# Mean squares of a fused block kernel: one product with a matrix of 1/n and a logarithm-exponential factor, in place of token sums, square root, reciprocal and spread

## The chip, the cores and the metric

The kernel runs on one core of a Trainium2 chip. The metric is the device time of one execution in microseconds (us); less is better. Times of the kernel before are a median of three runs. TensorE (PE) multiplies matrices, VectorE (DVE), ScalarE (ACT) and GpSimd (POOL) work elementwise, and SyncE (SP) issues most of the transfers.

## The reference

Two transformer blocks stand one after the other, for one sequence of 512 tokens and 1024 channels, in float32. What matters here are their root mean square norms:

```python
def rmsnorm(t, g):
    y = t * lax.rsqrt(jnp.mean(t * t, axis=-1, keepdims=True) + EPS)   # EPS = 1e-6
    return y * g
```

They stand at these places:

- the first block's input norm (not touched here)
- a norm without weights of each of the 4 retention heads over its 512 value channels ("r")
- the first block's second norm, ahead of its feed-forward part ("n2")
- the first block's final norm over 1024 channels, and right behind it the second block's input norm ("n3" and "n3x"; see below)
- a norm of each of the 4 heads of the gated linear attention (GLA) over 128 channels ("g")
- the second block's norm ahead of its feed-forward part ("n4")
- the final norm (not touched here)

Around the norms stand projections of 1024 by 1024 and more, stick-breaking attention, retention, GLA, an attention over selected keys, and two gated feed-forward parts.

## The kernel before

**Layout.** Activations lie with channels on the 128 partitions and tokens along the free dimension: a tile is 128 channels by 512 tokens. A norm's sum over channels is then a sum over partitions, which TensorE makes, and the factor of each token must stand on all 128 partitions to multiply such tiles.

**Products.** Each big product is computed from operands split in a high and a low part: three matmuls of 512 columns (lines L1468, L1469, L1471) for each weight tile of 128 by 128. The weights are read in blocks into three buffers `stg` by SP. ScalarE rounds half a block into `wh` (L2223, 128x1024), and VectorE or GpSimd subtracts it into `wl` (L1767, L2578). A `split` in the order is this pair. Matmuls on plain float32 tiles stand in the trace as two records each.

**Order.** The class `Plan` writes one list of operations by hand-set rules, and every engine executes its own items of that list in order, with semaphores between engines. Foreground jobs are the big products. Side work is written as generators (`retain` for a retention head, `factors3` for n3 and n3x, `gla`, `turn_x` for n4) that advance one `yield` at a time between the weight tiles of the products: a stage has a rate, such as 0.55 or 1.1 steps for each tile. `rest(m)` or `pause=m` lets m such steps go by. `norm2` has no such cover: the next product is of the normed tile itself.

**A norm before.** ScalarE or GpSimd and VectorE have squared and added the channel tiles into one or two tiles of 128x512.

1. TensorE sums over partitions with the squares as stationary operand: four matmuls of one column (`token_sums` at L1570 for r and g; `sums` at L1602 and L1606, once for the accumulated tile and once for the last tile). The result is one value for each token, tokens on partitions, 128x4.
2. `sprd`: ScalarE loads the table of square roots (L2332) and takes the root of 128x4 (L2345), VectorE takes the reciprocal (L1888) and writes four diagonal tiles of 128x128 (L1895).
3. `sprdm`: TensorE multiplies them with a matrix of ones, four matmuls of 128 columns (L1585), which puts the factor on all partitions of a bank.
4. The readers: `rn` (L1901), `n2` (L1943), `x3` (L2010), `gn` (L2107); for n3 and n4 `rt` (L2003) copies the factor into the tile `RT`, by which the next products are multiplied as they leave their banks.

n3 folds two norms: `m1` makes the first one's mean times EPS, and the factor of the second follows from both sums. `tmt` (L2441) wants n3's factor with tokens on partitions, `rt3`, a copy of the 128x4 value.

**Around n2.** The order there is: squares of the last tile, `sums`, `sprd`, `sprdm`, `a2` (a small VectorE operation, L1934), a block's load, one `split`, and then `n2` and `n2_low` for the eight channel tiles (L1943 on VectorE, L2206 on ScalarE, L1954 on VectorE). The first product follows as its operands come.

**Around g.** The generators of the key selection (`best`, L2053 and L2055 on VectorE, ending with `chosen`, L2059) and of the GLA are interleaved; the attention (`al` at L1697) follows.

Of the kernel before, what the change touches and what calls it, by code (L numbers as in the profile page):

```python
# [55 lines left out]
def constants():  # L56
# [13 lines left out]
    mats = np.stack([np.eye(P), np.ones((P, P)),  # L70
                     ((s <= t) & (s // 64 == t // 64)).astype(float)], 1)
# [6 lines left out]
class Plan:  # L78
# [6 lines left out]
    def __init__(self):  # L85
# [5 lines left out]
        self.of = {}  # L91
# [158 lines left out]
def make_plan():  # L250
# [105 lines left out]

    def attend(pr):
# [9 lines left out]

        def rest(m):
            for _ in range(m):
                yield  # L370
# [104 lines left out]
    def spread(key, n, pause=0):  # L475
        emit("sprd", key, n)
        p.of["sprd", key] = p.counts["sprd"]
        for _ in range(pause):
            yield
        emit("sprdm", key)  # L480

    def retain(hh):
# [14 lines left out]
        take("O", ("r", hh), 2)  # L497
        emit("rsum", hh)
        yield from spread(("r", hh), 512, pause=6)
        yield  # L500
# [84 lines left out]
    def sums(which, f):  # L585


        emit("square", which, f)
        if f == KT - 1:
            def add():  # L590
                take("O", which)
                emit("sums", which)
            p.later.append([1, add])
# [35 lines left out]
    def norm2():  # L629
        p.flush()  # L630
        for _ in spread("n2", D):
            pass
# [120 lines left out]
    def factors3():  # L753
        yield
        yield
        p.flush()
        emit("m1")
        yield from spread("n3", D, pause=7)
        emit("rt", "n3")
# [3 lines left out]
        take("O", "n3x")  # L763
        yield from spread("n3x", D, pause=7)
# [77 lines left out]
    def gla():  # L842
        def rest(m):
            for _ in range(m):
                yield

# [37 lines left out]
        for r in range(2):  # L884
# [8 lines left out]
            for hh in range(2):  # L893
# [11 lines left out]
                take("O", ("g", hd), 2)  # L905
                emit("gsum", hd)
                yield from spread(("g", hd), P, pause=5)
                yield
# [144 lines left out]
    def turn_x():  # L1053
# [3 lines left out]
        yield from spread("n4", D, pause=10)  # L1057
        emit("rt", "n4")
# [23 lines left out]
v_set cact ada pe_ada a_x v_x v_a1 a_n1 sba sbr v_rot p_rot v_rs a_rsq p_rsq a_spread v_spread v_rn v_gr  # L1082
a_sq v_sq pe_sum v_a2 v_n2 v_m1 v_extra v_x3 v_sc v_best a_gb v_gc a_gd v_gd a_ge p_gf a_gg p_gh a_gh p_gi
# [16 lines left out]
def program(nc, a, out, scratch):  # L1100
# [8 lines left out]
    with base:  # L1109
# [8 lines left out]
        matf = sb("matf", [P, 2, P])  # L1118
# [7 lines left out]
        ONES, ONEC = matf[:, 0, :], matf[:, 0, 0:1]  # L1126
# [11 lines left out]
        m1c, m1s, top8, decs, fs, fd, fr = (cell(n) for n in (4, 4, 8, 16, 8, 4, 4))  # L1138
        mx, nmx, rsm = cell(32), cell(32), cell(32)
        vw = [(cell(4), cell(4)) for _ in range(2)]  # L1140
# [15 lines left out]
        with ExitStack() as ph:  # L1156
# [4 lines left out]
            with ExitStack() as ph1:  # L1161
# [4 lines left out]
                rdiag = sb("rdiag", [P, S], ctx=ph1)  # L1166
# [101 lines left out]
        def diag_of(key):  # L1268
            if isinstance(key, tuple):
                return rdiag if key[0] == "r" else tmp9  # L1270
            return TMP[6]

        def sums_of(key):
            ob = BANK[7]
            if isinstance(key, tuple):
                return ob[:, 0:4]
            if key == "n3x":
                return m1s
            return ob[:, 4:8] if key == "n3" else ob[:, 0:4]
# [74 lines left out]
        def sync(eng):  # L1354
# [6 lines left out]
            def row_load(k):  # L1361
# [5 lines left out]
                if k == 2:  # L1367
                    nc.sync.dma_start(matf[:, :, :], a["k_mats"][:, 1:3, :]).then_inc(s["d_matf"], 16)
# [40 lines left out]
        def tensor(eng):  # L1409
# [157 lines left out]
            def token_sums(key, sq):  # L1567
                ob = free(pe, key)
                for i in range(4):
                    t = T.matmul(ob[:, i:i + 1], sq[:, i * P:(i + 1) * P], ONEC, start=True, stop=True)  # L1570
                t.then_inc(fill(key), 1)

            def rsum(hh):
                pe.wait_ge("p_rsq", 3 * (hh + 1))
                token_sums(("r", hh), SQ)

            def gsum(hd):
                pe.wait_ge("a_gsq", hd + 1)
                token_sums(("g", hd), tmp8)

            def sprdm(key):
                ob, dg = free(pe, key), diag_of(key)
# [1125 lines left out]
```

## Time and profile before

| | us |
|---|---|
| median of three runs | 1940.64 (1938.31 to 1940.73) |
| the profiled execution, its device time | 1939.97 |
| its span, first to last instruction | 1938.2 |
| PE busy | 1894.5 |
| VectorE busy | 883.9 |
| ScalarE busy | 676.5 |
| GpSimd busy | 515.8 |

The mean granted TensorE clock of the profiled execution is 0.991 of full speed. The span is the profile's, and what is worked out below in microseconds of the span is taken off the device time of the same execution, which is 1.8 us longer than its span.

### The profile page before, as it was taken

Reading aid. Unit: us, or ns where it says so; the run is one execution under the profiler, and the core shown is the slowest. Engines: PE = TensorE matmul, PEld = TensorE weight load, DVE = VectorE, ACT = ScalarE, POOL = GpSimd, SP = SyncE. Lnnn points to the kernel's source line nnn. Section 1 sums busy time; section 2 is a strip of 40 time slices with the busy share of each in tenths; the row PEclk is TensorE's granted clock in tenths of the full one; section 3 lists DMA queues with packets and bytes.
Section 4 is the critical chain, followed back from the end, with each engine's and each line's share of the span. In section 5 each row is a group of like instructions: output and inputs, shape, how many; then the busy total and the mean of one; then the engine's idle time right before and its main releaser. Section 6 shows DMA issues by size and latency. Waiting matters only on the chain.

```text
span 1938.2 us, 21970 instructions
## 1 busy us (share of the span) xinstructions
PE 1894.5 (98%) x8837; PEld 1486.7 (77%) x8837; DVE 883.9 (46%) x1416; ACT 676.5 (35%) x1009; POOL 515.8 (27%) x285
## 2 busy tenths in 40 slices
PE   7999999999999999989999999999999999999998
PEld 6777778877777778877888888877676778888886
DVE  6466542655261314343333333557477654423433
ACT  5555541223232322433222223425336432212223
POOL 3433334444353533410000000134245311100100
PEclk9999999999999999989999999999899999999999
DMA  9411214534442123324323222423112132322321
GB/s 300 139 45 65 66 66 142 173 112 150 131 143 96 66 87 109 103 71 126 104 82 111 90 84 77 118 77 97 44 57 78 52 98 88 108 87 87 105 91 44
DMA packets 182332, 192.35 MB, mean 99 GB/s; under 512 B 10154, under 2 KB 166192, under 8 KB 181976
## 3 DMA queue, kind: packets, MB, share of 16 engines
q1 hardware_dynamic: 179704, 180.71, 29.2%
q0 software_dynamic: 1104, 5.24, 1.0%
q10 hardware_dynamic: 1424, 5.00, 0.7%
q8 instruction: 71, 1.16, 0.3%
q14 instruction: 29, 0.24, 0.0%
HBM read 188.82 MB, written 4.72 MB: 100 GB/s over the span
## 4 chain that ended last, share of the span: by engine, by line
PE 88%; DVE 8%; ACT 2%; issue 1%; POOL 1%; DMA 0%; DVEq 0%; SPq 0%; ACTq 0%; POOLq 0%
PE bank L1468 24%; PE bank L1471 23%; PE bank L1469 23%; PE bank L1490 2%; PE bank L1489 2%; PE bank L1488 2%; PE bank L1564 2%; DVE left L1827 2%; PE bank L1498 1%; PE bank L1534 1%; PE bank L1550 1%; PE bank L1514 1%; DVE ADA L1785 1%; PE bank L1450 1%; PE bank L1451 1%
## 5 line engine op out<-in xcount | busy, mean ns | idle before, releaser
L2578 POOL TENSOR_TENSOR wl<-stg,wh 128x1024 fp32r<-128x1024 f32 x150 | 364.6, 2432 | 865.3 <-ACT wh L2223 865.2
L1468 PE MATMUL bank<-hH,wh 128*128 128x512 f32 x1264 | 521.3, 412 | 2.8 <-DVE hL L1954 2.5
L1471 PE MATMUL bank<-hH,wl 128*128 128x512 f32 x1264 | 503.1, 398 | 0.0
L1469 PE MATMUL bank<-hL,wh 128*128 128x512 f32 x1264 | 502.9, 398 | 0.0
L2223 ACT ACTIVATE wh<-stg 128x1024 fp32r<-128x1024 f32 (+2 forms) x292 | 298.5, 1024 | 286.7 <-PE bank L1471 204.9
L1468 PEld LDWEIGHTS bank<-hH,wh 128*128 128x128 f32 x1264 | 239.9, 190 | 72.0 <-issue 19.3
L1471 PEld LDWEIGHTS bank<-hH,wl 128*128 128x128 f32 x1264 | 239.4, 189 | 58.1
L1469 PEld LDWEIGHTS bank<-hL,wh 128*128 128x128 f32 x1264 | 240.5, 190 | 51.1 <-issue 0.7
L1767 DVE TENSOR_TENSOR wl<-stg,wh 128x1024 fp32r<-128x1024 f32 (+2 forms) x142 | 168.1, 1186 | 238.0 <-ACT wh L2223 237.5
L1468 PE MATMUL bank<-h2H,wh 128*128 128x512 f32 x352 | 140.9, 400 | 0.0
L1471 PE MATMUL bank<-h2H,wl 128*128 128x512 f32 x352 | 140.2, 398 | 0.0
L1469 PE MATMUL bank<-h2L,wh 128*128 128x512 f32 x352 | 140.2, 398 | 0.0
L2626 POOL TENSOR_TENSOR tmp<-tmp,SQ 128x512 f32<-128x512 f32 x22 | 28.5, 1296 | 298.0 <-ACT tmp L2407 298.0
L1785 DVE SCALAR_TENSOR_TENSOR ADA<-stg,small,ADA 128x256 f32<-128x256 f32 x112 | 79.7, 712 | 3.4
L1471 PEld LDWEIGHTS bank<-h2H,wl 128*128 128x128 f32 x352 | 66.7, 190 | 16.2
L1468 PEld LDWEIGHTS bank<-h2H,wh 128*128 128x128 f32 x352 | 66.7, 190 | 15.8
L1469 PEld LDWEIGHTS bank<-h2L,wh 128*128 128x128 f32 x352 | 66.6, 189 | 15.9
L1971 DVE TENSOR_TENSOR tmp<-bank,tmp 128x512 f32<-128x512 f32 x44 | 30.4, 691 | 91.3 <-PE bank L1471 91.3
L1471 PE MATMUL bank<-fHa,wl 128*128 128x512 f32 x176 | 69.8, 396 | 0.0
L1468 PE MATMUL bank<-fHa,wh 128*128 128x512 f32 x176 | 69.8, 396 | 0.0
L1469 PE MATMUL bank<-fLa,wh 128*128 128x512 f32 x176 | 69.8, 396 | 0.0
L1827 DVE TENSOR_TENSOR_SCAN left<-tmp,masks 128x384 f32<-128x384 f32 (+2 forms) x64 | 61.9, 998 | 0.0
(328 smaller groups left out, 2616.4 us busy)
## 6 DMA issues: line engine op xcount, KB each, us to landing
stg<-in_w_in SPq DMA_DIRECT2D x54, 1024.0 KB, 5.2
stg<-in_w_ffn_in SPq DMA_DIRECT2D x22, 1024.0 KB, 5.1
stg<-in_w_ada SPq DMA_DIRECT2D x16, 1024.0 KB, 5.3
stg<-in_w_ffn_gate SPq DMA_DIRECT2D x11, 1024.0 KB, 5.2
stg<-in_w_ffn_up SPq DMA_DIRECT2D x11, 1024.0 KB, 5.3
stg<-in_w_ffn_down SPq DMA_DIRECT2D x10, 1024.0 KB, 5.0
stg<-in_w_ada SPq DMA_DIRECT2D x16, 512.0 KB, 6.2
stg<-in_w_proj_ret SPq DMA_DIRECT2D x8, 1024.0 KB, 5.0
```

What stands on the lines that cost most here:

```text
L1468: T.matmul(ps, wh, xh, start=j["first"] and k == 0, stop=False)
L1469: T.matmul(ps, wh, xl, start=False, stop=False)
L1471: t = T.matmul(ps, wl, xh, start=False, stop=j["stop"] and last)
L1488: T.matmul(gb[:, :], xh, wh, start=s0, stop=False)
L1489: T.matmul(gb[:, :], xh, wl, start=False, stop=False)
L1490: t = T.matmul(gb[:, :], xl, wh, start=False, stop=s1)
L1564: t = T.matmul(cb[:, j * P:S], v[:, j, d * P:(d + 1) * P], TMP[4 + n][:, off:off + w], start=j == 0, stop=j == 3)
L1767: V.tensor_tensor(lo, src, hi, ALU.subtract).then_inc(s["w_lo_dve"], 1)
L1785: V.scalar_tensor_tensor(last, view[:, k, :], cact[:, k:k + 1], acc, ALU.mult, ALU.add).then_inc(s["ada"], 1)
L1827: t = V.tensor_tensor_scan(left[:, back], tt[:, back], masks[:, 3, back], 1.0, ALU.mult, ALU.add)
L2223: A_.activation(hi, src, ACTF.Copy).then_inc(s["w_hi"], 1)
L2578: G.tensor_tensor(lo, src, hi, ALU.subtract).then_inc(s["w_lo_pool"], 1)
```

## The change

The constant `ones` becomes three constant matrices filled with 1/1024, 1/512 and 1/128. One matmul of 512 columns with such a matrix as stationary operand and the squares as moving operand puts the mean square of each token on all 128 partitions of a bank. Where `sums` had two groups of four one-column matmuls for each tile of squares, it has two such matmuls. The factor is then `exp(-0.5 * ln(mean + EPS))`: two ScalarE operations over 128x512, the first from the bank into a tile (`rlog`, `tmp9`, TMP[6] or TMP[4]), the second back into the bank, or for n3 and n4 straight into `RT`, so `rt` goes. `sprd`, `sprdm`, the reciprocal and the diagonals go. The table of both functions is loaded explicitly for r and g; for n2, n3 and n4 ahead of time, behind the square of channel tile 6. `m1` becomes two VectorE operations over 128x512. `rt3` is made by four one-column matmuls on `RT` and a small ScalarE copy. n3x takes a bank of its own (ring C), and `rt3` one of ring Z. The pauses in the order change as shown.

```diff
-    mats = np.stack([np.eye(P), np.ones((P, P)),
-                     ((s <= t) & (s // 64 == t // 64)).astype(float)], 1)
+    means = [np.full((P, P), 1.0 / n) for n in (D, 512, P)]
+    mats = np.stack([np.eye(P), *means, ((s <= t) & (s // 64 == t // 64)).astype(float)], 1)
...
     def retain(hh):
-        take("O", ("r", hh), 2)
+        take("O", ("r", hh))
         emit("rsum", hh)
-        yield from spread(("r", hh), 512, pause=6)
-        yield
+        yield from rest(2)
+        factor(("r", hh))
+        yield from rest(2)
...
     def norm2():
         p.flush()
-        for _ in spread("n2", D):
-            pass
+        factor("n2")
...
     def factors3():
         p.flush()
+        yield from rest(4)
         emit("m1")
-        yield from spread("n3", D, pause=7)
-        emit("rt", "n3")
+        yield
+        factor("n3")
         give("n3")
         p.known.add("r2")
         yield
-        take("O", "n3x")
-        yield from spread("n3x", D, pause=7)
+        factor("n3x")
+        yield from rest(2)
+        take("Z", "rt3")
+        emit("rt3")
+        give("rt3")
...
     def gla():
-                yield from spread(("g", hd), P, pause=5)
-                yield
+                yield from rest(2)
+                factor(("g", hd))
+                yield from rest(2)
...
     def turn_x():
-        yield from spread("n4", D, pause=10)
-        emit("rt", "n4")
+        yield from rest(3)
+        factor("n4")
...
             def rsum(hh):
+                pe.wait_ge("d_matf", 16)
                 pe.wait_ge("p_rsq", 3 * (hh + 1))
-                token_sums(("r", hh), SQ)
+                ob = free(pe, ("r", hh))
+                T.matmul(ob[:, :], MEAN[512], SQ[:, :], start=True, stop=True).then_inc(fill(("r", hh)), 1)
...
             def rt3_(*_):
+                zb = free(pe, "rt3")
+                emptied(pe, "n3")
                 for i in range(4):
+                    t = T.matmul(zb[:, i:i + 1], RT[:, i * P:(i + 1) * P], ident[:, 0:1], start=True, stop=True)
...
             def sums(which):
+                for ob, (acc, _) in zip(banks, SQS[which]):
+                    T.matmul(ob[:, :], MEAN[D], acc[:, :], start=True, stop=False)
                 pe.wait_ge("a_sq", squared(which, KT - 1))
+                for key, ob, (_, tt) in zip(keys, banks, SQS[which]):
+                    T.matmul(ob[:, :], MEAN[D], tt[:, :], start=False, stop=True).then_inc(fill(key), 1)
...
             def m1():
+                m = TMP[6][:, :]
+                V.tensor_scalar(m, filled(ve, "n3x")[:, :], EPS, EPS * EPS, ALU.mult, ALU.add).then_inc(s["v_m1"], 1)
+                ve.wait_ge("v_m1", 1)
+                V.tensor_tensor(m, filled(ve, "n3")[:, :], m, ALU.add).then_inc(s["v_m1"], 1)
...
+            def factor(key):
+                if isinstance(key, tuple):
+                    A_.preload_act_table_set("natural_log_exp_and_others")
+                log = log_of(key)
+                if key == "n3":
+                    ac.wait_ge("v_m1", 2)
+                    A_.activation(log[:, :], log[:, :], ACTF.Ln).then_inc(s["a_log"], 1)
+                else:
+                    ob = filled(ac, key)
+                    A_.activation(log[:, :], ob[:, :], ACTF.Ln, bias=e6).then_inc(s["a_log"], 1)
+                ac.wait_ge("a_log", of["log", key])
+                if key == "n3" or key == "n4":
+                    A_.activation(RT[:, :], log[:, :], ACTF.Exp, scale=-0.5).then_inc(empty(key), 1)
+                else:
+                    A_.activation(ob[:, :], log[:, :], ACTF.Exp, scale=-0.5).then_inc(s["a_log"], 1)
```

## Rows read from the trace of the kernel before

**Rows 1.** The page: busy time by engine; the chain that ended last, by engine.

```profile
PE 1894.5 (98%) x8837; PEld 1486.7 (77%) x8837; DVE 883.9 (46%) x1416; ACT 676.5 (35%) x1009; POOL 515.8 (27%) x285
PE 88%; DVE 8%; ACT 2%; issue 1%; POOL 1%; DMA 0%; DVEq 0%; SPq 0%; ACTq 0%; POOLq 0%
```

**Rows 2.** Busy us (count) by stretch: PE, PEld, DVE, ACT, POOL; clock, DMA, GB/s.

```profile
24.00:60.00 36.00, 35.86 (x174) 29.55 (x173) 24.77 (x63) 19.72 (x30) 25.96 (x18) 1.00 1.01 286
400.00:740.00 340.00, 337.52 (x1490) 264.43 (x1490) 128.09 (x210) 101.35 (x136) 148.40 (x73) 1.00 0.32 106
857.00:872.00 15.00, 10.09 (x43) 8.44 (x42) 10.87 (x20) 7.41 (x10) 0.00 (x0) 0.66 0.19 66
1242.00:1256.00 14.00, 14.00 (x76) 12.15 (x76) 5.81 (x20) 7.05 (x9) 6.13 (x3) 0.88 0.30 96
1362.00:1382.00 20.00, 18.01 (x62) 12.91 (x62) 6.28 (x14) 4.81 (x7) 2.35 (x1) 0.66 0.17 53
1552.00:1564.00 12.00, 11.06 (x54) 9.00 (x53) 6.99 (x13) 6.08 (x7) 0.00 (x0) 0.86 0.46 148
```

**Rows 3.** The chain around retention head 0: start us, us, what.

```profile
400.74 1.72 PE bank L1550 x4
...
425.98 0.79 PE bank L1570 x8
...
433.89 0.89 PE bank L1585 x8
```

**Rows 4.** The timeline around n2: start us, us, engine, operation, idle before.

```profile
858.45 0.63 ACT L2388 ACTIVATE tmp<-XR 128x512 f32<-128x512 f32 x1 [3.99 <-DVE XR L1930]
...
859.09 1.28 ACT L2332 ACT_TABLE_LOAD   x1
...
859.13 1.05 PE L1606 MATMUL bank<-small,tmp 128*128 128x1 f32 x8 [0.72 <-ACT tmp L2388]
860.39 0.26 ACT L2345 ACTIVATE small<-bank,small 128x4 f32<-128x4 f32 x1
860.55 1.05 ACT L2223 ACTIVATE wh<-stg 128x1024 fp32r<-128x1024 f32 x1
860.68 0.18 DVE L1888 RECIPROCAL small<-small 128x4 f32<-128x4 f32 x1 [2.27 <-ACT small L2345]
860.90 0.87 DVE L1895 TENSOR_SCALAR tmp<-ident,small 128x128 f32<-128x128 f32 x4
...
861.76 1.22 DVE L1767 TENSOR_TENSOR wl<-stg,wh 128x1024 fp32r<-128x1024 f32 x1
...
861.83 2.08 PE L1585 MATMUL bank<-tmp,matf 128*128 128x128 f32 x8 [1.65 <-DVE tmp L1895]
863.94 1.41 DVE L1943 SCALAR_TENSOR_TENSOR tmp<-XR,small,bank 128x512 f32<-128x512 f32 x2 [0.96 <-PE bank L1585]
```

**Rows 5.** The chain behind n2: products at half and at full clock.

```profile
867.64 0.43 PE bank L1471
...
871.09 0.23 PE bank L1471
```

**Rows 6.** Groups of ScalarE by form: one wide operation from a bank, one from SBUF.

```profile
L2487 ACT ACTIVATE tmp<-bank 128x512 f32<-128x512 f32 x4 | 2.4, 600 | 23.8 <-PE bank L1684 23.8
...
L2461 ACT ACTIVATE tmp<-tmp 128x512 f32<-128x512 f32 x2 | 1.3, 634 | 0.1
```

**Rows 7.** The chain at the sums of n3.

```profile
1242.91 1.68 PE bank L1602 x16
1244.59 2.03 PE bank L1606 x16
```

**Rows 8.** The chain at the first GLA head.

```profile
1374.46 1.50 PE bank L1570 x8
```

**Rows 9.** The timeline where the attention begins.

```profile
1441.83 2.06 DVE L2059 TENSOR_SCALAR SW<-SW 128x512 f32<-128x512 f32 x1
...
1444.70 0.70 PE L1697 MATMUL bank<-KA,QA 64*128 64x256 f32 x4 [1.23 <-DVE small L2122]
```

More of the change, by code:

```diff
@@ L355, in make_plan, with rest @@
     stage()
+    def rest(m):
+        for _ in range(m):
+            yield
     def attend(pr):
@@ L473, in rg_after @@
             p.fore.append(retain(hh))
[L475 to L478, printed above, removed]
-            yield
-        emit("sprdm", key)
+    def factor(key):
+        p.logs += 1
+        p.of["log", key] = p.logs
+        if key not in ("n3", "n4"):
+            p.logs += 1
+            p.of["factor", key] = p.logs
+        emit("factor", key)
     def retain(hh):
@@ L591, in add @@
                 take("O", which)
+                if which == "n3":
+                    take("C", "n3x")
                 emit("sums", which)
@@ L1266, in fkey, with log_of @@
             return ("f" + tag, t // FA), t % FA
-        def diag_of(key):
+        def log_of(key):
             if isinstance(key, tuple):
[L1270 to L1279, printed above, removed]
+                return rlog if key[0] == "r" else tmp9
+            return TMP[4 if key == "n3x" else 6]
         def fm_of(name, e):
@@ L1595, in sums @@
             def sums(which):
-                ob = free(pe, which)
-                pe.wait_ge("v_set", 2)
+                keys = ["n3x", "n3"] if which == "n3" else [which]
+                banks = [free(pe, key) for key in keys]
                 pe.wait_ge("v_sq", added(which, KT - 2))
-                for g, (acc, _) in enumerate(SQS[which]):
-                    for i in range(4):
-                        T.matmul(ob[:, 4 * g + i:4 * g + i + 1], acc[:, i * P:(i + 1) * P], one, start=g == 0 and i == 0, stop=False, skip_group_check=True)
+                for ob, (acc, _) in zip(banks, SQS[which]):
+                    T.matmul(ob[:, :], MEAN[D], acc[:, :], start=True, stop=False)
                 pe.wait_ge("a_sq", squared(which, KT - 1))
-                for g, (_, tt) in enumerate(SQS[which]):
-                    for i in range(4):
-                        t = T.matmul(ob[:, 4 * g + i:4 * g + i + 1], tt[:, i * P:(i + 1) * P], one, start=False,
-                                     stop=i == 3 and g == len(SQS[which]) - 1, skip_group_check=True)
-                t.then_inc(s["pe_sum"], 1)
+                for key, ob, (_, tt) in zip(keys, banks, SQS[which]):
+                    T.matmul(ob[:, :], MEAN[D], tt[:, :], start=False, stop=True).then_inc(fill(key), 1)
             def bias():
@@ L1878, in rvv, with factor @@
                 V.tensor_tensor(RG[:, d, :], cb[:, :], RG[:, d, :], ALU.mult).then_inc(empty(("rvv", hh, d)), 1)
[L1880 to L1895 removed]
+            def factor(key):
+                ve.wait_ge("a_log", of["factor", key])
+                return BANK[bank[key][0]]
             def rn(hh, d):
                 key = ("r", hh)
[L1899 removed]
+                rsb = factor(key)
                 emptied(ve, ("rvv", hh, d))
@@ L2104, in gn @@
                 key = ("g", hd)
-                rsb = filled(ve, key, 1)
+                rsb = factor(key)
                 emptied(ve, ("go", hd))
```

101 lines of the change are left out of this document (28 added, 73 removed).

## The prediction

> **What bounds the kernel now.** I read the page first: TensorE is busy for 1894.5 of 1938.2 us and holds 88% of the chain that ended last [rows 1]. So time on TensorE counts nearly one for one, and time on ScalarE or VectorE counts only where TensorE waits for it. Next I read the windows by stretch, because they show where TensorE is not at its full rate. In the retention stage (400 to 740 us) it is busy 337.5 of 340 us at clock 1.00; around n2, at n3, in the GLA and at n4 the granted clock falls to means of 0.66, 0.88, 0.66 and 0.86 [rows 2]. The half level is 1.2 GHz, the full one 2.4. Last I read the chain and the timeline at each norm: what a norm costs TensorE, and, for n2, who waits for whom.
>
> A product's matmul takes 0.43 us at half clock and 0.23 to 0.24 at full [rows 5], so of each us at half clock 0.45 us is lost. The time at half clock in a stretch is twice its length times (1 - mean clock): 2 x 14 x 0.12 = 3.4 us at n3, 2 x 12 x 0.14 = 3.4 us at n4, 2 x 20 x 0.34 = 13.6 us in the GLA, 2 x 15 x 0.34 = 10.2 us around n2 [rows 2].
>
> **The price of the new product.** A plain float32 matmul of 512 columns is priced by the scores of a retention head: two of them, on full tiles, take 1.72 us on the chain [rows 3], so 0.86 us each. The old four one-column matmuls take 0.79 us and the spread's four of 128 columns 0.89 us [rows 3].
>
> **Retention heads.** 0.79 + 0.89 - 0.86 = 0.82 us less of TensorE each, 3.3 us for four. TensorE has no slack there, so this counts in full. ScalarE gets a logarithm from a bank (0.60 us) and an exponential (0.63 us) [rows 6] for a root of 0.26 us [rows 4], about 1 us more per head; the table loads stay one per head. ScalarE is busy for 101 of 340 us in this stage [rows 2], which hides it. VectorE loses a reciprocal and four diagonals, 0.18 + 0.87 = 1.05 us at the least [rows 4]. If TensorE had waits to fill there, the gain could be anything down to nothing; the busy share says it has almost none.
>
> **GLA heads.** The same, 0.82 us, for three. The first head's sum ran at half clock, 1.50 us [rows 8]; there 1.50 + 0.89 - 2 x 0.86 = 0.67. Together 3.1 us.
>
> **n2, the only norm without cover.** I follow the chain. The last square ends at 859.08. Before, one-column matmuls, root, reciprocal, diagonals and spread follow, and the first `n2` starts at 863.94 [rows 4]. Now the last tile's matmul starts at 859.13 as before (the accumulated tile's one is done by then: TensorE had 0.72 us to wait for that square [rows 4], and 0.86 us is hardly more than the narrow group it replaces), and ends at about 860.2, with 0.2 us for its drain. Logarithm 0.60 and exponential 0.63 end at 861.45. If `n2` came then, 2.4 us would be won. But the order puts one `split` ahead of `n2`, and every engine is in order. Before, ScalarE rounded `wh` at 860.55 while VectorE was still at the reciprocal, and VectorE did `wl` from 861.76 to 862.98, under the spread matmuls (861.83 to 863.91) [rows 4]: both halves were free. Now ScalarE reaches `wh` only behind the exponential: 861.45 + 1.05 = 862.5, and VectorE's `wl`, which stands ahead of the first `n2` in its queue, ends at 863.7. So the first `n2` starts at about 863.7, and 0.2 us is won instead of 2.4. If the new matmul runs at half clock it is 0.86 us longer: 0.6 us lost. Bounds: -0.6 to +2.4, I take +0.2. The half clock behind n2 stays; I take it as it was. The table load of 1.28 us [rows 4], moved behind square 6, lies under a product of 24 x 0.235 = 5.6 us; without that cover it would cost its 1.28 us.
>
> **n3 and n3x.** Sums before: 1.68 + 2.03 = 3.71 us [rows 7], and two spreads, 1.78 us. Now four wide matmuls, 3.44 us, and four one-column ones for `rt3`, 0.79 us. 3.71 + 1.78 - 3.44 - 0.79 = 1.3 us less. The longer chain of `m1` (two wide VectorE operations) and four ScalarE operations is hidden under the next product, which does not need `RT` until its end, 5.6 us later; what is left over would cost what it overruns.
>
> Then the clock. Between 1242 and 1256 us TensorE is busy in all 14.00 us, and still the clock fell [rows 2]; the engine had just done 3.7 us of one-column matmuls [rows 7]. In the retention stage, with the float32 matmuls of up to 512 columns, it stood at 1.00 throughout. The new sums are such matmuls, so I expect the clock to stand. Of the 3.4 us at half clock, 0.7 us is in the 2.03 us already counted (2.03 - 1.68 is half of it); the other 2.7 us give back 2.7 x 0.45 = 1.2 us. n3 together: 2.5 us, bounds 1.3 and 2.5.
>
> **n4.** The spread's 0.89 us [rows 3] goes. Of the sums, the accumulated tile's matmul lies ahead of the wait for the last square, as before, and the last tile's takes about what the four narrow ones did. The clock fell behind these sums too: 3.4 x 0.45 = 1.5 us to be given back. Together 2.4 us, bounds 0.9 and 2.4.
>
> The Trainium skill bears on these two clock terms. Its page TensorE: Matmul & The Clock Gate, section on HAM oscillation, puts the fall down to stretches in which the engine idles. The trace does not agree at n3, where TensorE shows no idle time at all. By that rule n4, which keeps its short waits for the squares, would not be cured; that is rival 1.
>
> **Start of the attention.** The key selection ends with `chosen`, 1441.83 to 1443.89, and the second item of the attention waited 1.23 us for VectorE [rows 9]. The last two GLA heads no longer put 1.05 us or more each on VectorE ahead of it, 2.1 us, while TensorE arrives 1.6 us earlier by its own savings; later waits of the same kind shrink too. Fewer steps also pull the last selection steps forward in the order. I take 1.0 us, bounds 0 and 2.5.
>
> **The larger constant.** The load of the matrices grows from 128 to 256 KB at a time when the DMA share is 1.01 at 286 GB/s [rows 2]: 131 KB at that rate are 0.46 us. From 24 to 60 us TensorE is busy 35.9 of 36.0, so it does not wait for these transfers. I take 0, at most 0.46.
>
> **The sum.** 3.3 + 3.1 + 0.2 + 2.5 + 2.4 + 1.0 = 12.5 us. The profiled execution took 1939.97 us (span 1938.2), so 1927.5. The median is 0.67 above that execution: 1928.1. I say 1928.
>
> **Rivals.**
>
> 1. *The clock falls anyway at n3 and n4*, as the waits and the narrow `rt3` matmuls stay, and n2 meets the half clock with its wide matmul. The sum loses 1.2 + 1.5, 0.8 at n2 and the 1.0 of the attention: 8.0 us, so about 1932.5. For it: the clock also fell in stretches with waits, in the GLA. Against it: at n3 there was none, only narrow work.
> 2. *The GLA gets its clock back sooner.* The 13.6 us at half clock cost 6.1 us, and the first head's one-column sum lies in them, at 1374 [rows 8]. Without it the clock may return sooner; also what begins the fall comes at another moment. Worth 3 to 6 us: 1922 to 1925.
> 3. *Slower: the half clock of the GLA lasts on.* Its stretches of small matmuls are now met at other moments; if the clock, once down, stays down past 1382, each us costs 0.45. It decides from 12.5 / 0.45 = 28 us more, and up to the attention at 1441.8 [rows 9] (60 us more) it would cost 27 us, so up to 1955. Against it: on the same work the clock came back after 13.6 us before.
> 4. *TensorE's savings turn into waits* for ScalarE or VectorE, since ScalarE now sits in each norm for 1.28 + 0.60 + 0.63 us [rows 4, 6] and `rn` and `gn` come after fewer steps. VectorE would stand in front of other banks' readers. That gives 1936 to 1942. Against it: ScalarE's share of 35% [rows 1].
> 5. *The change doesn't do what it says*: logarithm and exponential each want a table load of their own, and the early load is lost. It shows in full only at n2, 2 x 1.28 = 2.6 us [rows 4]: 1930.5. The Trainium skill (ScalarE: Activation LUTs, section on table sets) has both functions in one set; in this trace the exponential and logarithm of the GLA's gates follow each other with 0.1 us between them [rows 6], so it agrees.
>
> **How the numbers follow.** Forecast 0.53 (with rival 5, 0.03, inside its own range 1924.5 to 1931), rival 1 0.18, rival 2 0.14, rival 4 0.07, rival 3 0.05. The range 1922 to 1934 leaves out rivals 3 and 4 and a third of rival 2, with a little of rival 1. About 0.2% (3.9 us) is what a measurement of this kernel can tell from no change. Faster: 0.53 + 0.03 + 0.18 + 0.14 and a little of rival 4, 0.89. Same: 0.06. Slower: 0.05.
>
> **What would show it.** In the new profile: the mean matmuls at about 0.86 us on the chain; clock 1.00 behind the sums of n3 and n4; at n2 exponential, `wh`, `wl`, `n2` in a row with no idle time between them, and TensorE idle from 860.2 relative until the first product; retention with no wait of TensorE. It would be wrong with a clock lower in the GLA than 0.66 or for longer, with TensorE waiting behind `gn` or `rn`, or with more table loads than the code asks for.

## The result

| | before | after |
|---|---|---|
| median, us | 1940.28 (four runs, 1938.31 to 1940.73) | 1922.47 (four runs, 1922.06 to 1923.94) |
| the profiled execution, device time | 1939.97 | 1923.94 |
| its span | 1938.2 | 1922.1 |
| its mean granted clock | 0.991 | 0.993 |

The ratio of after to before is 0.9912 (95% interval 0.9894 to 0.9929): 17.8 us less by the medians, 16.0 us by the two profiled executions. The forecast was 12.5 us less (1928.0), and the range 1922 to 1934 holds the result near its low end. So the sign is right and about 4 us of the profiled execution, over 5 us of the median, are to be found beside the forecast.

The page of after, the rows that answer to [rows 1]:

```profile
PE 1879.3 (98%) x8653; PEld 1463.2 (76%) x8653; DVE 868.0 (45%) x1352; ACT 687.2 (36%) x1021; POOL 516.4 (27%) x285
PE 87%; DVE 8%; ACT 2%; issue 2%; POOL 1%; DMA 0%; ACTq 0%; DVEq 0%; SPq 0%; POOLq 0%
```

TensorE lost 15.2 us of busy time and is still the bound; VectorE lost 15.9 us and ScalarE gained 10.7 us. The windows of after, at the places that answer to [rows 2] (columns: stretch, length, busy us and count of PE, PEld, DVE, ACT, POOL, then clock, DMA share, GB/s):

```profile
400.00:740.00 340.00, 338.86 (x1457) 263.14 (x1456) 126.57 (x194) 106.11 (x140) 151.81 (x74) 1.00 0.33 108
857.00:872.00 15.00, 12.16 (x44) 9.71 (x45) 11.17 (x17) 5.72 (x8) 0.00 (x0) 0.77 0.00 0
1234.00:1248.00 14.00, 13.79 (x57) 9.74 (x56) 9.85 (x15) 8.84 (x13) 6.21 (x3) 1.00 0.32 95
1353.00:1374.00 21.00, 18.87 (x60) 12.48 (x59) 5.75 (x10) 6.32 (x9) 2.35 (x1) 0.67 0.16 51
1536.00:1548.00 12.00, 11.15 (x46) 7.84 (x45) 6.87 (x9) 8.90 (x11) 1.30 (x1) 1.00 0.40 131
```

Read the clock column: at n3 (third row) and n4 (last row) it is 1.00 where it was 0.88 and 0.86, although TensorE is busy for a little less of each stretch than before. In the GLA (fourth row) 2 x 21 x 0.33 = 13.9 us at half clock are left, as before (the windows' rounded clocks make 13.6 to 13.9 us of one and the same length). At n3 and n4 the clock stood at 1.00 in the profiled execution of every kernel below too.

**Where the 16.0 us came from.** The same matmuls, those of the retention, the GLA and the attention, are found in both traces by their tiles; the difference of their start times, after less before, is the gain up to there.

| stretch | gain | forecast |
|---|---|---|
| start, up to the first products | 1.4 | 0 |
| the four retention heads: 1.57, 1.58, 0.95, 0.9 | 5.0 | 3.3 |
| n2 | 0.0 | 0.2 |
| n3 and n3x | 2.1 | 2.5 |
| GLA up to the attention | 5.1 | 3.1 + 1.0 |
| attention to the end, with n4 | 2.4 | 2.4 |

The 1.4 us at the start is not the change's. The same transposes of the input, in code that the change leaves alone, took 6.69 us in the profiled execution before and 5.40 us in this one; in the kernels below, whose start is the same code too, they took 5.62 to 6.62 us. The other 1.8 us between the two medians are not in this table: the three further runs of after took 1922.06 to 1922.53 us at mean clocks of 0.994 and 0.995, against 0.993 in the profiled one, and the third group below shows where a difference of this size lies.

TensorE's own busy time over the retention and over the GLA, between the same matmuls, first before and then after (length, busy us and count, clock, DMA share, GB/s):

```profile
400.60:741.58 340.98, 338.50 (x1495) 1.00 0.32 105
1276.37:1444.72 168.35, 163.60 (x801) 0.96 0.22 69
```

```profile
399.19:735.14 335.95, 334.81 (x1439) 1.00 0.33 107
1267.84:1431.10 163.26, 159.76 (x744) 0.96 0.22 71
```

In the retention 3.7 us of the 5.0 are less work of TensorE, 0.92 us a head, and 1.3 us are less waiting. In the GLA 3.8 us of the 5.1 are less work, 0.96 us a head, and 1.3 us less waiting.

### The profile page after: what moved, and what is told of

The parts are those of the page before. It is cut to its first block, busy times and chain, and to the rows that moved or that the text cites. A ratio compares the mean times of both kernels' runs of the same rounds, so it can differ in the third digit from the quotient of the medians.

```text
span 1922.1 us, 21539 instructions
## 1 busy us (share of the span) xinstructions
PE 1879.3 (98%) x8653; PEld 1463.2 (76%) x8653; DVE 868.0 (45%) x1352; ACT 687.2 (36%) x1021; POOL 516.4 (27%) x285
## 4 chain that ended last, share of the span: by engine, by line
PE 87%; DVE 8%; ACT 2%; issue 2%; POOL 1%; DMA 0%; ACTq 0%; DVEq 0%; SPq 0%; POOLq 0%
PE bank L1465 23%; PE bank L1468 23%; PE bank L1466 23%; PE bank L1487 2%; PE bank L1486 2%; PE bank L1485 2%; PE bank L1561 2%; DVE left L1819 2%; PE bank L1495 1%; DVE ADA L1777 1%; PE bank L1531 1%; PE bank L1547 1%; PE bank L1511 1%; PE bank L1447 1%; PE bank L1448 1%
## 5 line engine op out<-in xcount | busy, mean ns | idle before, releaser
L2200 ACT ACTIVATE wh<-stg 128x1024 fp32r<-128x1024 f32 (+2 forms) x292 | 298.3, 1024 | 283.6 <-PE bank L1468 202.8
L1777 DVE SCALAR_TENSOR_TENSOR ADA<-stg,small,ADA 128x256 f32<-128x256 f32 x112 | 88.7, 792 | 3.7
```

The costliest lines, as they stand in the source:

```text
L1777: V.scalar_tensor_tensor(last, view[:, k, :], cact[:, k:k + 1], acc, ALU.mult, ALU.add).then_inc(s["ada"], 1)
L2200: A_.activation(hi, src, ACTF.Copy).then_inc(s["w_hi"], 1)
```

## n2, as it came out

The timeline of after around n2, which answers to [rows 4]:

```profile
852.03 0.63 ACT L2367 ACTIVATE tmp<-XR 128x512 f32<-128x512 f32 x1 [2.57 <-DVE XR L1909]
...
852.71 1.12 PE L1600 MATMUL bank<-tmp,matf 128*128 128x512 f32 x2 [0.64 <-ACT tmp L2367]
853.87 0.69 ACT L2315 ACTIVATE tmp<-bank,small 128x512 f32<-128x512 f32 x1 [1.22 <-PE bank L1600]
854.59 0.60 ACT L2320 ACTIVATE bank<-tmp 128x512 f32<-128x512 f32 x1
855.13 1.04 ACT L2200 ACTIVATE wh<-stg 128x1024 fp32r<-128x1024 f32 x1
856.20 1.23 DVE L1759 TENSOR_TENSOR wl<-stg,wh 128x1024 fp32r<-128x1024 f32 x1 [4.13 <-ACT wh L2200]
857.34 1.40 DVE L1922 SCALAR_TENSOR_TENSOR tmp<-XR,small,bank 128x512 f32<-128x512 f32 x2
...
859.84 0.76 PE L1465 MATMUL bank<-hH,wh 128*128 128x512 f32 x1 [6.00 <-DVE hL L1933]
```

From the square's end (852.66) to `n2` (857.34) it takes 4.68 us; before it took 4.86 us, from 859.08 to 863.94 [rows 4]. So the new form, whose own matmul, logarithm and exponential end at 855.19, wins 0.2 us and not 2.4, as forecast: what stands between is `wh` and `wl` of the one split, in VectorE's and ScalarE's order. TensorE's idle time at the first product grows from 2.5 to 6.0 us, since the spread's work (2.08 us) and the waits around it are no longer there to fill it.

The chain right behind shows where the 0.2 us went again:

```profile
863.59 0.43 PE bank L1468
864.01 0.42 PE bank L1465
864.43 0.23 PE bank L1466
```

The products run at half clock from 859.84 to 864.43, 4.59 us; before from 866.45 to 870.63, 4.18 us. 0.41 us more at half clock is 0.2 us. The half-clock time as a whole fell from 10.2 to 2 x 15 x 0.23 = 6.9 us, but what vanished lay under an idle TensorE, where the clock costs nothing, and under the spread's matmuls, which are gone in any case.

## Experiments

Each kernel is the kernel after with the edit shown, unless said. Kernels of one group ran on one chip beside runs of the kernel before. "Offset" is the start time of the same matmul, the kernel's less that of after. The ratio is to the kernel before on the same chip.

### First group: which part paid what

Before here: median 1941.92.

**VectorE's old work put back at the retention heads** (the sums stay new; the result of the added work is not used):

```diff
+            def rsum(i):
+                ve.wait_ge("v_bal", 5 * i)
+                V.reciprocal(bal, col[:, 56:60]).then_inc(s["v_bal"], 1)
+                ve.wait_ge("v_bal", 5 * i + 1)
+                for c in range(4):
+                    V.tensor_scalar(rdiag[:, c * P:(c + 1) * P], ident[:, :], bal[:, c:c + 1], None, ALU.mult).then_inc(s["v_bal"], 1)
```

> The changed kernel with VectorE's old work for the retention heads put back as ballast: at each rsum a reciprocal of 128x4 and four diagonals of 128x128 into a tile nobody reads, without the waits. Theory: the change saved about 0.75 us at each of heads 0 and 1 beyond TensorE's own 0.82 us, because the sums of w_ada that follow on VectorE end sooner and TensorE waits less for them (1.1 us in all after, 2.5 us before). Then this run gives back 1.4 to 1.5 us against the changed kernel, and TensorE's wait for ADA is near 2.5 us again. Rival: the 0.75 us came from the shorter pauses or from VectorE no longer waiting for the root; then the ballast costs under 0.3 us and the wait stays near 1.1 us.

Median 1925.29 (1923.12 to 1925.47), ratio 0.9911 (0.9894 to 0.9927). The offset grows by 0.96 us at head 0 and by 0.79 us at head 1, and by nothing at heads 2 and 3. Where the time goes stands in the list of TensorE's waits (what it waited for: us in total, times, longest). First the kernel before, then after, then this kernel:

```profile
PE bank L1428 <- DVE ADA L1785: 2.5, 2, 1.2
```

```profile
PE bank L1425 <- DVE ADA L1777: 1.1, 2, 0.6
```

```profile
PE bank L1427 <- DVE ADA L1779: 2.3, 2, 1.3
```

`ADA` are the sums over `w_ada` that VectorE accumulates for the one-column matmuls of `adasum`; they run beside heads 0 and 1 alone. So at these two heads TensorE waited for VectorE, and in the order of the changed kernel the old work of VectorE would cost 0.96 + 0.79 = 1.75 us: the theory's number, and not the rival's.

That doesn't make the reciprocal and the diagonals the cause of the wait in the kernel before. At head 0 that wait ends at 450.94, 20 us behind the diagonals. VectorE in between, in the kernel before:

```profile
437.68 0.69 DVE L1859 TENSOR_TENSOR rk<-bank,cosr 128x512 f32<-128x512 f32 x1 [0.78 <-PE bank L1471]
...
442.96 0.67 DVE L1901 TENSOR_TENSOR rg<-rg,bank 128x512 f32<-128x512 f32 x1
443.56 0.68 DVE L1750 TENSOR_TENSOR orL<-rg,orH 128x512 fp32r<-128x512 f32 x1
```

And after:

```profile
432.19 1.28 DVE L1880 TENSOR_TENSOR rg<-rg,bank 128x512 f32<-128x512 f32 x2
...
437.37 0.68 DVE L1851 TENSOR_TENSOR rk<-bank,cosr 128x512 f32<-128x512 f32 x1
...
440.35 7.46 DVE L1777 SCALAR_TENSOR_TENSOR ADA<-stg,small,ADA 128x256 f32<-128x256 f32 x7
```

Before, VectorE stood idle at 437.68 until TensorE's product was there, so whatever it was late by from the diagonals was gone. Behind that point five operations of the head's readers (`rn` at L1901 and its low part at L1750, about 3.0 us) stood among the sums that TensorE waited for. After, with fewer steps, the readers come from 432.19 on, ahead of `rk`, and the sums follow each other. So the trace gives the shorter wait to the order with fewer steps. This order needs VectorE without the old work, as the ballast shows: from the start of head 0's sums to their end VectorE waits nowhere for TensorE. The changed sums with the old pauses were not tried, so the two are not parted by a run. At head 1 both orders are the same as here.

The old work also took very unequal times. VectorE at that place, first the kernel before and then this one:

```profile
428.63 2.81 DVE L1895 TENSOR_SCALAR rdiag<-ident,small 128x128 f32<-128x128 f32 x4
```

```profile
427.75 0.88 DVE L1883 TENSOR_SCALAR rdiag<-ident,small 128x128 f32<-128x128 f32 x4
```

The last section comes back to this.

**The same work put back at the GLA heads.** The same diff, for `gsum` and with a tile `gdiag`.

> The same ballast at each gsum of the GLA in place of the retention heads. Theory: of the 5.1 us won between n3 and the attention, 3.1 us are TensorE's own and up to 2 us are VectorE's relief; the ballast gives back 0.7 to 2 us, at the waits of TensorE for VectorE where the attention begins. Rival: these 2 us come from the order with fewer steps; then the ballast costs under 0.3 us.

Median 1922.48 (1922.11 to 1923.71), ratio 0.9901 (0.9887 to 0.9916). The waits at the end of the GLA are the same to a tenth:

```profile
PE bank L1674 <- DVE tmp L2086: 2.1, 1, 2.1
PE bank L1691 <- DVE small L2108: 0.5, 1, 0.5
```

Outside the stretch at half clock no head loses anything. So VectorE's relief, one of the two causes by which I had explained the 1.0 us of the attention's start, is worth nothing there in the new order. But this execution was 3.2 us ahead of after's by the end of the GLA's half clock, which the next window shows: 2 x 23 x 0.15 = 6.9 us at half clock, against 13.9.

```profile
1351.00:1374.00 23.00, 20.52 (x84) 14.27 (x84) 9.87 (x21) 9.66 (x14) 4.08 (x3) 0.85 0.15 46
```

Whether the ballast did that is asked again in the second and third groups.

**The kernel before with wider matmuls in its sums**: 64 equal columns in place of one, read back with a stride. Nothing else of the change is in it.

```diff
-                        T.matmul(ob[:, 4 * g + i:4 * g + i + 1], acc[:, i * P:(i + 1) * P], one, start=g == 0 and i == 0, stop=False, skip_group_check=True)
+                        j = 64 * (4 * g + i)
+                        T.matmul(ob[:, j:j + 64], acc[:, i * P:(i + 1) * P], ONES[:, 0:64], start=g == 0 and i == 0, stop=False, skip_group_check=True)
...
```

> The kernel before, with only the width of its sums for n2, n3 and n4 changed: each one-column matmul becomes 64 columns wide (64 equal columns of the matrix of ones), at nearly the same price on the chain. Theory: the narrow matmuls let the clock fall at n3 and n4; now it stays at 1.00 there and the kernel is 2.5 to 3 us faster than the kernel before. Rival, by the rule that only idle time lowers the clock: the idle time is unchanged, the clock falls as before, and the time is that of the kernel before within 0.5 us.

Median 1936.40 (five runs, 1932.61 to 1937.77), ratio 0.9968 (0.9955 to 0.9981). The windows at n3 and n4, and the sums of n3 on the timeline:

```profile
1241.00:1255.00 14.00, 14.00 (x87) 12.32 (x86) 6.56 (x21) 6.93 (x9) 7.13 (x3) 1.00 0.32 96
1550.00:1562.00 12.00, 11.12 (x60) 9.10 (x59) 7.59 (x13) 7.39 (x10) 0.00 (x0) 1.00 0.51 154
```

```profile
1242.12 1.00 PE L1603 MATMUL bank<-matf,SQ 128*128 128x64 f32 x8
...
1242.95 1.06 PE L1603 MATMUL bank<-matf,tmp 128*128 128x64 f32 x8
...
1243.85 1.95 PE L1608 MATMUL bank<-matf,tmp 128*128 128x64 f32 x16
```

The wide groups cost no more than the narrow ones: the first two together run from 1242.12 to 1243.85, 1.73 us, against 1.68 [rows 7]. But the clock stays at 1.00 at both places, where it was 0.88 and 0.86, and n3 comes out 1.57 us shorter and n4 1.5 us. The TensorE waits at n4 are those of before (0.7 us for the last square), so the idle time didn't change, only the width of the matmuls. That is the forecast's mechanism by itself, with its two clock terms (1.2 and 1.5 us), and it speaks against rival 1.

The clock by place is known from one profiled execution of each. The mean clocks of all runs go the same way: 0.989 or 0.990 in the 22 runs of the kernel before in the three groups, 0.992 to 0.994 in the five of this one. The times have more in them than n3 and n4. The profiled execution is 2.2 us faster than that of the kernel before: 1.57 + 1.5 us there and 0.5 us at n2, less 1.5 us for a longer half clock in the GLA (17.1 us). The median is 5.5 us lower than beside it, more than the 2.5 to 3 us expected; the mean clocks differ by about 0.003, and half clock of 3.4 us at each of n3 and n4 makes 0.0018 of that. Where the rest lay in these runs isn't known.

**The split behind the second `n2`.**

```diff
-        p.prepare(p.ahead)
         for k in range(KT):
             ...
+            if k == 1:
+                p.prepare(p.ahead)
```

> The changed kernel with the one split that stands ahead of n2 moved behind the second channel tile. Theory: wh and wl stand between the exponential and the first n2; without them the first n2 starts 2.2 us sooner after the last square, and the kernel is about 2 us faster than the changed one (half clock behind n2 may move it by 1 us either way). Rival: the third product of the trio then waits for wl, or n2_low is pushed back behind wl, and TensorE loses there what it won: within 0.5 us of the changed kernel.

Median 1922.89 (1922.83 to 1922.97), ratio 0.9902 (0.9888 to 0.9917). The timeline:

```profile
855.13 0.69 ACT L2316 ACTIVATE tmp<-bank,small 128x512 f32<-128x512 f32 x1 [1.22 <-PE bank L1601]
855.85 0.60 ACT L2321 ACTIVATE bank<-tmp 128x512 f32<-128x512 f32 x1
856.49 1.41 DVE L1923 SCALAR_TENSOR_TENSOR tmp<-XR,small,bank 128x512 f32<-128x512 f32 x2 [3.16 <-ACT bank L2321]
...
858.99 0.77 PE L1466 MATMUL bank<-hH,wh 128*128 128x512 f32 x1 [3.90 <-DVE hL L1934]
```

`n2` now stands right behind the exponential, the wait falls from 6.0 to 3.9 us, and the offset falls by 2.25 us at n2 (from +1.26 to -0.99). The median doesn't show it: this execution was 1.26 us behind after's from the start, and its GLA had 13.8 us at half clock (2 x 23 x 0.30), where that of the GLA's ballast kernel beside it had 6.9. The third group shows it.

### Second group: prices and the GLA

Before here: median 1940.90.

**The mean matmul of the retention heads issued twice.**

```diff
+                T.matmul(ob[:, :], MEAN[512], SQ[:, :], start=True, stop=True)
                 T.matmul(ob[:, :], MEAN[512], SQ[:, :], start=True, stop=True).then_inc(fill(("r", hh)), 1)
```

> The changed kernel with each of the four retention heads' mean matmuls issued twice into the same bank. Theory: one costs TensorE 0.86 us and nothing hides it, so the offset against the changed kernel grows by 0.86 us at each head, 3.4 us in all. Rival: TensorE waits there anyway (for the sums of w_ada at heads 0 and 1), and part of it is free: under 2.5 us.

Median 1924.55 (two runs, 1923.28 and 1925.82), ratio 0.9915. The offset grows by 0.30, 0.07, 0.90 and 0.86 us at heads 0 to 3. At heads 2 and 3 this is the price forecast for such a matmul, 0.86 us, which the chain of after shows too:

```profile
636.95 0.86 PE bank L1569 x2
```

At heads 0 and 1 the second matmul costs much less, and the wait for `ADA` is gone from the list: TensorE does there what it waited for otherwise. It is 2.1 us in all and not 3.4, so the theory missed and the rival came. Together with the first kernel this settles it for the order of after: at these two heads VectorE's sums set the pace, not TensorE.

**Two more steps of the generator behind the factor in the GLA**, as many as the kernel before needed.

```diff
                 factor(("g", hd))
-                yield from rest(2)
+                yield from rest(4)
```

> The changed kernel with two more steps between the factor and gn of each GLA head, so six between sum and gn as before. Theory: about 1.9 us of the 5.1 us won in this stage come from the order with fewer steps, as TensorE's waits for VectorE there fell from 3.9 to 2.6 us; with the steps back, 1 to 2 us are lost and the waits return. Rival: the place in the order is nothing, and what fell was VectorE's wait at the reciprocal: under 0.3 us.

Median 1923.52 (two runs, 1923.26 and 1923.78), ratio 0.9909. Its GLA had 6.9 us at half clock, as that of the two kernels with ballast (the second one is next). But where their offset falls by 3.24 and 3.25 us over the GLA, its own falls by 2.05: the added steps cost 1.2 us. The list of waits says where:

```profile
PE bank L1689 <- DVE small L2099: 1.6, 1, 1.6
```

This is the wait at the start of the attention: 1.2 us in the kernel before [rows 9], 0.5 us in after. Fewer steps between the heads pull the key selection's last steps forward in the order, and in the changed kernel that is worth 1.2 us. Against the kernel before this wait is shorter by 0.7 us.

**The ballast of the GLA with a wait too** (VectorE waits for the sum's matmul ahead of the reciprocal):

```diff
             def gsum(i):
+                filled(ve, ("g", i))
                 ve.wait_ge("v_bal", 5 * i)
```

> The changed kernel with VectorE's reciprocal and four diagonals put back for the GLA heads, and now also a wait of VectorE for the sum's matmul, as the reciprocal had (it waited 10.1 us in four times for ScalarE's root before). Theory of the wait: it holds up what stands behind it in VectorE's queue, and 1 to 2 us come back at TensorE's waits for tmp and small. Rival (the steps): with the ballast alone nothing came back, and with the wait neither does: under 0.3 us. A GLA stretch at half clock of another length is left out of the comparison, by the offsets outside it.

Median 1922.22 (1922.21 and 1922.22), ratio 0.9903. No wait of TensorE changes and no head loses time, though VectorE now stands for 7.6 us in four times ahead of the reciprocal. In the kernel before it was 10.1 us, as there it waited for ScalarE's root, which is not in this kernel. A wait of 7.6 us so costs TensorE nothing in this order.

**Both repairs, first try**: the later split, and the early table load one square sooner (behind square 5) at n2, n3 and n4.

```diff
-                if f == KT - 2:
+                if f == KT - 3:
                     A_.preload_act_table_set("natural_log_exp_and_others")
```

> The changed kernel with the split ahead of n2 moved behind the second channel tile, and the early table load moved from square 6 to square 5. The first won 2.2 us at n2; the second should remove TensorE's wait of 0.2 us for the squares of n3, as the table load of 1.28 us no longer stands ahead of the last tile on ScalarE. Together 2.4 us faster than the changed kernel on the same chip. Rival: the table load at square 5 holds up ScalarE at another tile and nothing is won beyond 2.2 us.

Median 1920.46 (1919.69 to 1922.26), ratio 0.9895 (0.9878 to 0.9911). The reason for the edit stands on the timeline of after at n3:

```profile
1234.26 1.28 ACT L2369 ACT_TABLE_LOAD   x1
...
1235.55 1.06 ACT L2200 ACTIVATE wh<-stg 128x1024 fp32r<-128x1024 f32 x1
...
1236.51 0.71 ACT L2183 ACTIVATE hH<-XR,small 128x512 fp32r<-128x512 f32 x1
...
1237.13 0.61 ACT L2367 ACTIVATE tmp<-XR 128x512 f32<-128x512 f32 x1
```

ScalarE goes through them without a gap, and the chain of after runs through table load, `wh` and squares into the sums at 1238.40. So ahead of n3 the load is not hidden: it and all behind it make TensorE late. One square sooner gains 0.48 us at n3. At n4 it does harm:

```profile
PE bank L1598 <- DVE tmp L1981: 1.6, 1, 1.6
```

There the accumulated tile's matmul now waits 1.6 us for the last addition, where after waits 0.2 us, and 1.4 us are lost between the attention and the end.

### Third group: the same kernel again, and the best one

Before here: median 1940.79.

**The kernel after, unchanged.**

> The changed kernel once more, unchanged, on the chip of the next two. It says how much of a difference between two executions is chance: I expect the transposes at the start to take 5.4 to 6.7 us, the half clock behind n2 6.8 or 10.2 us, that in the GLA 6.8 or 13.7 us, and the median within 1.5 us of 1922.5, with the clock at 1.00 at n3 and n4.

Median 1921.95 (1921.61 to 1922.76), ratio 0.9902 (0.9887 to 0.9917). Its GLA:

```profile
1351.00:1374.00 23.00, 20.52 (x86) 14.39 (x84) 9.35 (x16) 9.99 (x15) 3.76 (x3) 0.85 0.15 46
```

Again 6.9 us at half clock and 3.2 us ahead of the first profiled execution by the GLA's end, with no edit at all. So the length of the GLA's half clock differs between executions of one program, and the ballast had no part in it. Nor does the chip decide it: each of the three groups, on three chips, has kernels with 6.9 us and kernels with 13.7. Of the ten kernels of these experiments that are built on the one after, six had 6.9 us there in the profiled execution and four 13.8 us; the kernel before with wide sums had 17.1 us.

**The later split, and the early load one square sooner at n3 alone.**

```diff
-                if f == KT - 2:
+                if f == (KT - 3 if which == "n3" else KT - 2):
```

> The changed kernel with the split behind the second channel tile of n2, and the early table load at square 5 for n3 only. At n4 the load at square 5 made TensorE wait 1.6 us for the sums' tile; at n3 it won 0.5 us. Theory: 2.2 + 0.5 = 2.7 us faster than the changed kernel, with no wait of 1.6 us for VectorE's tmp. Rival: the wait of 1.6 us belonged to n2 and stays, and only about 1.3 us is left.

Median 1920.21 (1918.98 to 1921.33), ratio 0.9892 (0.9878 to 0.9907): the fastest of all. Beside the unchanged kernel of this group, whose GLA had the same clock, its span is 2.5 us shorter (1917.5 against 1920.0) and the median 1.7 us. The 2.7 us of the theory are near the span's difference. The offset falls by 2.1 us at n2 and by 0.47 us at n3, and the wait of 1.6 us at n4 isn't there. The four runs of each don't overlap (1918.98 to 1921.33 against 1921.61 to 1922.76).

**That, with fewer steps around the GLA's factor.**

```diff
-                yield from rest(2)
+                yield from rest(1)
                 factor(("g", hd))
-                yield from rest(2)
+                yield from rest(1)
```

> The kernel before this one in the list, with one step in place of two ahead of and behind the factor of each GLA head. Two more steps had cost 1.2 us, at the wait of the attention's second item (1.6 us for 0.5 us). Theory: that wait of 0.5 us goes too, so 0.5 us faster. Rival: gn now waits for the exponential, as the table load, logarithm and exponential take 2.5 us, and VectorE stands: 0 to 1 us slower.

Median 1921.44 (1920.36 to 1922.17), ratio 0.9897 (0.9880 to 0.9913). It isn't faster. Its span is 2.9 us longer. The GLA's half clock of 13.8 us (2 x 23 x 0.30) is worth 3.2 of them; at n2 its half clock was shorter, 3.3 us against 6.6 (clock 0.89 against 0.78 over 15 us), which gives some back. And the wait at the start of the attention is 0.6 us longer, on which the clock has no bearing:

```profile
PE bank L1690 <- DVE small L2100: 1.1, 1, 1.1
```

The expectation that fewer steps are always better missed: two were enough, and one is too early. The rival's wait is there: VectorE waited 4.9 us in two times for the exponential ahead of `gn`, against 2.4 us in the kernel before this one in the list. But the 0.6 us above is all that TensorE is seen to lose by it.

## Why the prediction came out as it did

**Direction and bound: right.** TensorE was the bound and stayed it. Rivals 3 to 5 did not come: the clock came back in the GLA; TensorE's waits for VectorE and ScalarE fell at the heads and at the attention, and grew only at n2, as forecast, and by 0.2 us at n3; and the trace of after has the table loads that the code asks for, eight for r and g, three early ones. (Rival 5's own time is a slip: 1928.1 + 2.6 is 1930.7, not 1930.5.) Of the signs named, one was not met: retention still has a wait of TensorE, 1.1 us.

**Retention, 3.3 us forecast, 5.0 measured: the largest miss.** The step was "TensorE has no slack there, so this counts in full". Its TensorE part is right but small: 0.95 and 0.9 us at heads 2 and 3, 0.92 us a head over all four, for the 0.82 forecast. At heads 0 and 1 the busy share of 99% over 340 us hid two waits of 1.2 us. They are in the list of TensorE's waits of the kernel before, as 2.5 us for `ADA`. I read the mean and not the list. What the step put at nothing is 2.5 - 1.1 = 1.4 us less of these waits. VectorE's relief alone would not have given them, as the kernel before let VectorE stand idle between the diagonals and these sums; the readers that fewer steps brought ahead of the sums are in the trace of after what shortened them (first kernel of the experiments). The prediction counted fewer steps at the attention only.

**GLA, 3.1 + 1.0 forecast, 5.1 measured.** TensorE's part is 3.8 us and not 3.1: 0.96 us a head, as in the retention. Why a head gives some 0.1 us more than the sum of its matmuls on the chain was not looked for. The other 1.3 us are waits. The one at the attention's start fell from 1.2 to 0.5 us. I had argued 1.0 us for it, by two causes, VectorE's relief and fewer steps in the order. The ballast shows 0 for the first, the added steps 1.2 us for the second. The other is 0.5 us: of the two waits for `tmp`, the tile of the GLA's masked scores (2.7 us, twice, before; 2.1 us, once, after), the one at the third head is gone. The ballasts and the two added steps don't bring it back; what removed it was not tried by itself. So of the 1.0 us forecast for the attention's start 0.7 is found there, and the sum of this stage is off by TensorE's own part.

**n2, 0.2 forecast, 0 measured.** Its steps came out one by one: matmul, logarithm, exponential, `wh`, `wl`, `n2`. Moving the split gave 2.25 us more, which with the 0.2 makes the 2.4 of the upper bound. The 0.2 us went to 0.4 us more of products at half clock.

**n3, 2.5 forecast, 2.1 measured.** The clock stood, as forecast (1.2 us). What answers for the missing 0.4 us is the early table load, which I had hidden under "a product of 5.6 us". It lies under TensorE's product, but ScalarE has the squares to bring in the same time, and every operation behind the load is late by its 1.28 us. One square sooner gives 0.48 us back.

**n4, 2.4 forecast, 2.4 measured**, with the clock at 1.00. Here the load behind square 6 is rightly placed.

**Rival 1 fell.** At n3 TensorE was busy for 14.00 of 14 us before, and the clock fell; in the kernel before with 64-column sums it was busy as long and the clock stood. At n4 the waits for the squares are still there in after, 0.69 and 0.16 us, and it stood too. The Trainium skill, TensorE: Matmul & The Clock Gate, section on HAM oscillation, names idle stretches as the cause; here the waits of n4 alone didn't bring the fall, and with the wider matmuls it was gone.

**Rival 2 came in part, and by chance.** The GLA's half clock was as long as before in the profiled execution (13.9 us) and half of it in others, with a saving of 3.2 us then. The removal of the one-column sum is not what decides it, since one and the same program has both. The 16.0 us of the profiled execution are 3.5 more than the 12.5 forecast: 1.4 at the start, 1.7 in the retention, 1.0 in the GLA, less 0.2 at n2 and 0.4 at n3. The start is chance. So is, as far as the mean clocks tell, the further 1.8 us by which the median is lower than that.

## What to carry to other kernels

A busy share near 100% over hundreds of microseconds doesn't say that an engine never waits: read the list of its waits for the stretch, and ask of each whether the change shortens what it waits for. The order is part of a change: where fewer steps let one engine's operations move, look at what they now stand ahead of and behind. Matmuls of one column are dear twice here, by their own time and by the clock that fell behind them; the same sum over 64 columns cost the same and kept it. Where an operation is moved under a product, check the engine that executes it too: what is free on TensorE's side can stand in front of that engine's next due item, as the table load did at n3 and the split at n2.

## What was not expected of the hardware

- The clock fell behind narrow matmuls with TensorE busy the whole time: 0.88 with one column, 1.00 with 64 columns, in the same order of work and at the same time per group (1.68 and 1.73 us). These were 3.7 us of them in a row; the single groups of 0.79 us at the retention heads left it at 1.00.
- After a fall in the GLA the half clock lasts 6.9 us in some executions of one program and 13.7 us in others, worth 3.2 us, 0.17% of the kernel. One profile can't be compared with another below that size without a look at this stretch.
- VectorE's small operations become several times longer beside a large one of GpSimd. Four of 128x128 took 0.87 us at n2, where GpSimd was idle [rows 2, 4], and 2.81 us at retention head 0, where GpSimd made a `wl` (from 428.19, 2.58 us). After has the same with the sums of `ADA`, mostly 0.50 us each on the chain, but the one that fell beside `wl` 2.52 us:

```profile
427.87 2.55 POOL L2559 TENSOR_TENSOR wl<-stg,wh 128x1024 fp32r<-128x1024 f32 x1 [1.03 <-ACT wh L2200]
```

```profile
427.68 0.50 DVE ADA L1777
428.20 2.52 DVE ADA L1777
430.75 0.50 DVE ADA L1777
```

The late `ADA` ended at 430.72, 0.30 us after GpSimd's operation (430.42); the diagonals of the kernel before ended at 431.44, 0.67 us after theirs (430.77). The Trainium skill (SBUF — State Buffer, section Who interferes with whom) has a pair of ports that VectorE and GpSimd share as an exclusive lock, where the second to come waits until the first is done. These rows agree with it, but no run tried it by itself. An operation of VectorE can so take three times its usual time, or five. But its removal doesn't win that: the next operation takes the place beside `wl`. At head 0 VectorE needed 7.8 us before, from its operation `mod` (426.64) to the last of these sums (434.44), and 7.0 us after (425.24 to 432.27). That is 0.8 us less, though the reciprocal and the diagonals that went had taken 3.0.
